# Second expert stage of a two-block transformer kernel: inner columns dealt to partitions in runs of eleven

## The chip, the cores and the metric

The kernel runs on one core of one Trainium2 chip. The metric is the device time of one execution in microseconds (us); lower is better. Engines: PE is TensorE's matmul, PEld its weight load, DVE VectorE, ACT ScalarE, POOL GpSimd, SP the engine whose queue issues most DMAs. L12 is line 12 of the kernel.

## The reference

Two transformer blocks run over 256 tokens of width 1024, all in f32. The first has 32 experts of inner width 512. The second has a dense layer and then an expert layer with 8 experts of inner width 2816, two of them per token. The change touches only this last expert layer:

```python
def _moe_swiglu(u, w_router, w_gate, w_up, w_down):
    ...
    top_logits, top_idx = lax.top_k(logits, TOP_K)          # 2 of 8 experts
    top_w = jax.nn.softmax(top_logits, axis=-1)
    ...
    h = jax.nn.silu(lax.ragged_dot(xs, w_gate, group_sizes)) * lax.ragged_dot(xs, w_up, group_sizes)
    ys = lax.ragged_dot(h, w_down, group_sizes) * top_w.reshape(-1)[order][:, None]
    out = jax.ops.segment_sum(ys, tok, num_segments=n_tok)
```

w_gate and w_up are 8 x 1024 x 2816, w_down is 8 x 2816 x 1024. Their 277 MB are read from DRAM once.

## The kernel before, in words

Each expert is worked in two halves of its inner width: 1408 columns, as 11 tiles of 128 (TH = 11). A half is numbered n = 2e + v. The weights of a half are held in one region of SBUF (the ring of the earlier stages, used here as flat memory): held_gate and held_up hold four k-slices each (KQ = 4, 1408 columns each; a quarter), held_down holds 11 rows of 1024.

TensorE's program for a half (second_slots): half_in runs twice (kk = 0, 1) over the four gate slices and the four up slices. For each slice k it goes over the 11 tiles f of columns and two groups of 64 of them (c = 0, 1), with 64 weight columns as the stationary operand and the 80 token slots of the expert (x_rows) as the moving one. Such a slice, 22 matmuls, is called a piece here. half_down then takes the 11 rows f of held_down with the hidden values hid2 of the half before: 16 matmuls for each row (8 tiles of the output width, two groups of 64). Products are accumulated in PSUM: gate, up and y. After every odd half come the turning of y, the dispatch of the next expert's tokens and the combination into x. For each piece and for each row, TensorE raises the semaphore piece_used.

SP's queue loads the weights in a fixed order: for each half, the eight pieces of quarter 0, the 11 rows of down, and the eight pieces of quarter 1 (each expert: load_quarters, load_downs, load_quarters, twice). Before each DMA, SP waits until piece_used tells that the place is free. A piece is one DMA of 704 KB (128 partitions x 5632 bytes). A row of down is one DMA of 512 KB: partition p of row f receives row f x 128 + p of w_down's half, 4096 bytes; each of the 11 has its own semaphore down_row[f], on which TensorE waits before that row.

ScalarE copies x_rows for each slice (L746), applies silu to gate (L739); VectorE multiplies (L1466), clears PSUM (L1455), and does the combination (L1494, L1500, L1508). All matmuls are issued by the helper at L1824, the transposes by that at L1832.

There is a second form of the stage (second_all, for inputs where an expert gets more than 80 tokens). It does not run with these inputs; the change is made in it as well.

Of the kernel before, what the change touches and what calls it, by code (L numbers as in the profile page):

```python
# [13 lines left out]
P = 128  # L14
HALF = 64
D = 1024
KD = D // P
T = 256
# [23 lines left out]
FH = F2 // 2  # L42
TH = FH // P
KQ = KD // 2
QUARTER = KQ * FH
BANK_TILES = 6
PER_HALF = 4 * KQ + TH


def used_by(n, k):  # L50


    first = isinstance(n, int) and n == 0
    return n * PER_HALF + (k + 1 - (0 if first else TH))

# [73 lines left out]
def build(nc, a, out):  # L129
    with ExitStack() as ctx:  # L130
# [3 lines left out]
        def sem(name):  # L134
            return ctx.enter_context(nc.semaphore(name))
# [121 lines left out]
        x_rows = view(2048, KQ, CAP2)  # L257
# [6 lines left out]
        ps = ctx.enter_context(nc.psum_tensor("ps", [P, 8, CH], F32))  # L264
# [5 lines left out]

        gate_row = [sem(f"gate_row{k}") for k in range(KQ)]
        up_row = [sem(f"up_row{k}") for k in range(KQ)]
        down_row = [sem(f"down_row{f}") for f in range(TH)]
        piece_used = sem("piece_used")
        gate_clear, y_clear = sem("gate_clear"), sem("y_clear")
        rows_ready = sem("rows_ready")
# [48 lines left out]
        GATE_AT, UP_AT, DOWN_AT = 0, QUARTER, 2 * QUARTER  # L325
        held_gate = flat[:, GATE_AT:UP_AT].rearrange("p (k n) -> p k n", k=KQ)
        held_up = flat[:, UP_AT:DOWN_AT].rearrange("p (k n) -> p k n", k=KQ)
        held_down = flat[:, DOWN_AT:DOWN_AT + TH * D].rearrange("p (f n) -> p f n", f=TH)
# [30 lines left out]
        def _(sp):  # L359
# [32 lines left out]
            def expert_rows(w, e, c0, n):  # L392
                return w[bass.ds(e, 1), c0:c0 + n, :].rearrange("o (k p) n -> p (o k) n", p=P)
# [9 lines left out]
            w = a["w_in"][0]  # L403
# [57 lines left out]
            wg, wu, wd = a["moe_w_gate_2"][0], a["moe_w_up_2"][0], a["moe_w_down_2"][0]  # L461

            def left_by_ring(end):
                sp.wait_ge(ring_free, MOE2_SEQ - len(SUMMED) - SLOTS + 1 + (end - 1) // SLOT)
# [14 lines left out]

            def load_downs(e, v, n):  # L480

                for f in range(TH):
                    if n is None:
                        left_by_ring(DOWN_AT + (f + 1) * D)
                    else:
                        sp.wait_ge(piece_used, used_by(n - 1, 4 * KQ + f))
                    sp.dma_start(held_down[:, f, :], expert_rows(wd, e, v * FH, FH)[:, f, :]).then_inc(down_row[f], 16)

            load_quarters(0, 0, 0, None)
            load_downs(0, 0, None)  # L490
# [1324 lines left out]
        def _(pe):  # L1815
# [5 lines left out]
            def mm(*args, **kw):  # L1821


                ins = pe.matmul(*args, **kw)  # L1824
                if owed[0]:
                    ins.then_inc(owed_to[0], owed[0])
                    owed[0] = 0
                    return None
                return ins
# [196 lines left out]
            w = slot(s, KD, CH)  # L2026
            for g in range(2):
                bank = gv_()
                for i in range(2):
                    for k in range(KD):  # L2030
                        for half in range(2):
                            c0 = half * GROUP_HEADS * HD + (2 * g + i) * HD
                            last = mm(ps[half * HALF:(half + 1) * HALF, bank, i * T:(i + 1) * T], w[:, k, c0:c0 + HD],
                                      hT[:, k, :], start=(k == 0), stop=(k == KD - 1))
# [30 lines left out]
            for part in range(2):  # L2065
                turned = gv_()
                for i in range(4):
                    last = sums_turn(4 * part + i, turned, 4 * i)
# [9 lines left out]
            for t in range(TT):  # L2078
                bank = gv_()
                for g in range(4):  # L2080
                    last = mm(ps[:, bank, g * P:(g + 1) * P], gv[:, t, g * P:(g + 1) * P], wsT[:, g, :],
                                     start=True, stop=True)
                last.then_inc(v_full, 1)
            bank = gv_()
            for i in range(4):
                last = sums_turn(8 + i, bank, 4 * i)
# [4 lines left out]
            for g in range(6):  # L2091
# [3 lines left out]
                for i in range(nh):  # L2095
# [3 lines left out]
                    last = mm(ps[:, bank, i * keys:(i + 1) * keys], qT[base:base + HD, j, q0:q0 + P],  # L2099
                                     kT[base:base + HD, 0:keys], start=True, stop=True)  # L2100
# [11 lines left out]
            for blk in range(2):  # L2112
                pe.wait_ge(H["pT_ready"], 2 + 4 * blk)
                bank = gv_()
                for hd in range(HEADS):
                    base, kv = HD * (hd % 2), hd // GROUP_HEADS
                    dst = ps[base:base + HD, bank, (hd // 2) * P:(hd // 2 + 1) * P]
                    if blk == 0:
                        last = mm(dst, v_tok[:, 0, kv * HD:(kv + 1) * HD],
                                         pT[:, hd // 4, (hd % 4) * P:(hd % 4 + 1) * P], start=True, stop=True)  # L2120
                    else:
                        for kt in range(2):
                            at = (2 * (hd % 2) + kt) * P
                            last = mm(dst, v_tok[:, kt, kv * HD:(kv + 1) * HD],
                                             pT[:, 2 + hd // 2, at:at + P], start=(kt == 0), stop=(kt == 1))
# [99 lines left out]
            def second_all(q):  # L2225

                def part_in(n, kk):
                    for which, (w, full) in enumerate(((held_gate, gate_row), (held_up, up_row))):
                        for k in range(KQ):
                            pe.wait_ge(full[k], n * 32 + 16 * (kk + 1))  # L2230
                        for j, (lo, hi) in enumerate(dense_spans):
                            at = n * (4 * len(dense_spans)) + ((2 * kk + which) * len(dense_spans) + j)
                            if not isinstance(at, int) or at:
                                pe.wait_ge(sum_free, at)
                            for f in range(lo, hi):
                                for k in range(KQ):
                                    last = mm(ps[:, 4 + which, (f - lo) * T:(f - lo + 1) * T], w[:, k, f * P:(f + 1) * P],
                                              hT[:, kk * KQ + k, :], start=(k == 0), stop=(k == KQ - 1))
                            last.then_inc(sum_full, 1)
                        free(KQ, piece_used)  # L2240

                def half_in(n):
                    part_in(n, 0)
                    part_in(n, 1)

                def half_down(n, opens):
                    pe.wait_ge(q["hid_ready"], n)
                    for f in range(TH):
                        pe.wait_ge(down_row[f], n * 16)
                        for t in range(TT):  # L2250
                            for half in range(2):
                                last = mm(ps[:, 2 * t + half, :], dense_hid[:, f, t * P:(t + 1) * P],
                                          held_down[:, f, half * CH:(half + 1) * CH],
                                          start=(opens and f == 0), stop=(not opens and f == TH - 1))
                        last.then_inc(piece_used, 1)

                half_in(0)
                half_in(1)
                half_down(1, True)
                with pe.Fori(1, NE2) as i:  # L2260
                    half_in(i * 2)
                    half_down(i * 2, False)
                    half_in(i * 2 + 1)
                    pe.wait_ge(q["y_free"], i)
                    half_down(i * 2 + 1, True)
                half_down(2 * NE2, False)
                pe.wait_ge(q["y_free"], NE2)
# [95 lines left out]
            def second_slots(q, cap):  # L2363

                def quarter(w, full, n, kk, bank):
                    for k in range(KQ):
                        pe.wait_ge(rows_ready, n * (2 * KQ) + (kk * KQ + (k + 1)))
                        pe.wait_ge(full[k], n * 32 + (kk * 16 + 16))
                        for f in range(TH):
                            at = f % BANK_TILES * cap  # L2370
                            for c in range(2):
                                last = mm(ps[c * HALF:(c + 1) * HALF, bank + f // BANK_TILES, at:at + cap],
                                          w[:, k, f * P + c * HALF:f * P + (c + 1) * HALF], x_rows[:, k, :],
                                          start=False, stop=(k == KQ - 1), skip_group_check=True)
                        last.then_inc(piece_used, 1)
                    return last
# [8 lines left out]
                def half_down(n, y_cleared):  # L2385

                    pe.wait_ge(y_clear, y_cleared)
                    for f in range(TH):
                        pe.wait_ge(down_row[f], n * 16)
                        if f % BANK_TILES == 0:  # L2390
                            pe.wait_ge(q["hid_ready"], n * 2 + (f // BANK_TILES - 1))
                        for dt in range(KD):
                            for c in range(2):
                                last = mm(ps[c * HALF:(c + 1) * HALF, Y_BANK + dt // 4, (dt % 4) * cap:(dt % 4 + 1) * cap],
                                          held_down[:, f, dt * P + c * HALF:dt * P + (c + 1) * HALF],
                                          hid2[:, f * cap:(f + 1) * cap], start=False, stop=(f == TH - 1),
                                          skip_group_check=True)
                        last.then_inc(piece_used, 1)
# [102 lines left out]
            for layer in range(2):  # L2501
# [4 lines left out]
                if layer == 0:  # L2506
# [5 lines left out]
                    for c in range(9, ADA_CHUNKS):  # L2512
                        last = ada_turn(1, c, bank, 4 * (c - 8))
# [12 lines left out]
                w = slot(s, KD, CH)  # L2526
# [9 lines left out]
                for t in range(TT):  # L2536
                    last = mm(ps[:, bank, t * T:(t + 1) * T], glT[:, t * P:(t + 1) * P], gkw2[:, :],
                                     start=True, stop=True)
# [30 lines left out]
                for c in range(3):  # L2569
                    bank, rb, t = gv_(), CK * (c % 2), c // 2  # L2570
                    for hd in range(GH):
                        ob, f = DK * (hd % 2), hd // 2
# [119 lines left out]
```

## Time and profile before

| | us |
|---|---|
| median of 3 runs | 2091.62 |
| lowest, highest | 2085.76, 2098.47 |
| the profiled execution, in all | 2094.6 |
| its span | 2092.9 |

The mean granted clock of TensorE was 0.974 of full speed. The profile is one execution. Its page gives busy times and the chain that ended last; the trace behind it answers questions on a stretch, a line or a queue. "busy" of a group is the time in which at least one of its instructions ran; matmuls overlap, so their mean duration is much longer than the distance from one to the next, which is the busy time over their count. A row of the timeline is a run of like instructions: start, length, and the count behind the x; behind it, in brackets, the idle time before it and what ended it.

### The profile page before, as it was taken

Reading aid. Unit: us, or ns where it says so; the run is one execution under the profiler, and the core shown is the slowest. Engines: PE = TensorE matmul, PEld = TensorE weight load, DVE = VectorE, ACT = ScalarE, POOL = GpSimd, SP = SyncE. Lnnn points to the kernel's source line nnn. Section 1 sums busy time; section 2 is a strip of 40 time slices with the busy share of each in tenths; the row PEclk is TensorE's granted clock in tenths of the full one; section 3 lists DMA queues with packets and bytes.
Section 4 is the critical chain, followed back from the end, with each engine's and each line's share of the span. In section 5 each row is a group of like instructions: output and inputs, shape, how many; then the busy total and the mean of one; then the engine's idle time right before and its main releaser. Section 6 shows DMA issues by size and latency. Waiting matters only on the chain.

```text
span 2092.9 us, 67815 instructions
## 1 busy us (share of the span) xinstructions
PE 1985.1 (95%) x31049; PEld 1596.1 (76%) x31049; DVE 650.7 (31%) x1410; ACT 170.2 (8%) x370; POOL 17.3 (1%) x66
## 2 busy tenths in 40 slices
PE   6999899999999989999999999898999999999996
PEld 4787477877787757758677576688898989889894
DVE  4686332232232241354323523600211011110104
ACT  2002010000000011000000110110000000000000
POOL 1000000000000000000000000000000000000000
PEclk9999999999999999999999999999999999999997
DMA  9998559999999993346757433299999999999991
GB/s 351 320 389 311 227 202 418 421 421 422 424 421 421 422 370 144 121 143 249 272 206 262 180 108 133 99 413 384 402 359 379 416 365 413 375 370 412 360 358 74
DMA packets 179138, 655.98 MB, mean 313 GB/s; under 512 B 16212, under 2 KB 20724, under 8 KB 170868
## 3 DMA queue, kind: packets, MB, share of 16 engines
q1 hardware_dynamic: 170528, 647.41, 79.0%
q0 software_dynamic: 1456, 5.24, 0.7%
q10 hardware_dynamic: 7076, 2.20, 0.5%
q8 instruction: 60, 0.98, 0.2%
q14 instruction: 18, 0.15, 0.0%
HBM read 653.76 MB, written 1.05 MB: 313 GB/s over the span
## 4 chain that ended last, share of the span: by engine, by line
PE 89%; DVE 6%; DMA 2%; issue 2%; DVEq 0%; ACT 0%; SPq 0%
PE ps L1824 88%; DMA ring<-in_moe_w_gate_dram 2%; PE ps L1832 1%; DMA ring<-in_w_ada_dram 1%; DVE arena L1494 0%; DVE ps L1455 0%; DVE stat L1100 0%; DVE arena L1300 0%; DVE hT L988 0%; DVE x L1209 0%; DVE tok L975 0%; DVE x L1508 0%; DVE arena L1466 0%; DVE tok L1208 0%; DVE newton L968 0%
## 5 line engine op out<-in xcount | busy, mean ns | idle before, releaser
L1824 PEld LDWEIGHTS ps<-arena,ring 128*64 128x64 f32 (+1 forms) x25216 | 868.6, 139 | 46.2 <-issue 36.3
L1824 PE MATMUL ps<-arena,ring 128*64 128x80 f32 (+2 forms) x25216 | 885.8, 232 | 18.8 <-issue 15.0
L1824 PE MATMUL ps<-hT,ring 128*128 128x256 f32 (+1 forms) x1680 | 361.2, 387 | 4.3 <-DVE stat L992 2.2
L1824 PEld LDWEIGHTS ps<-hT,ring 128*128 128x128 f32 (+1 forms) x1680 | 309.4, 189 | 51.7 <-issue 2.6
L1824 PE MATMUL ps<-ring,arena 128*64 128x512 f32 (+1 forms) x880 | 273.8, 595 | 1.5 <-DVE stat L1732 1.1
L1824 PE MATMUL ps<-arena 128*128 128x128 f32 (+7 forms) x1288 | 231.9, 347 | 27.9 <-DVE x L1508 12.5
L1824 PEld LDWEIGHTS ps<-ring,arena 128*64 128x64 f32 (+1 forms) x880 | 104.5, 159 | 150.8 <-issue 147.2
L1824 PEld LDWEIGHTS ps<-arena 128*128 128x128 f32 (+4 forms) x1288 | 154.5, 191 | 84.9 <-issue 32.5
L1455 DVE MEMSET ps<- 128x480 f32 x68 | 28.9, 425 | 294.3 <-ACT arena L739 290.0
L1824 PE MATMUL ps<-ring,hT 128*128 128x512 f32 (+2 forms) x256 | 87.6, 500 | 0.0
L1824 PEld LDWEIGHTS ps<-ring,hT 128*128 128x128 f32 x256 | 46.1, 190 | 38.1 <-issue 36.2
L1373 DVE TENSOR_TENSOR arena<-arena,ps 128x256 f32<-128x256 f32 x32 | 13.5, 421 | 179.3 <-PE ps L1824 179.3
L1300 DVE SCALAR_TENSOR_TENSOR arena<-arena,csT 128x512 f32<-128x512 f32 x84 | 63.2, 752 | 3.0
L1057 DVE SCALAR_TENSOR_TENSOR arena<-ring,csT,arena 128x512 f32<-128x512 f32 x84 | 63.2, 752 | 3.0
L746 ACT ACTIVATE arena<-arena 128x80 f32<-128x80 f32 x96 | 25.9, 270 | 372.0 <-PE ps L1824 372.0
L1466 DVE TENSOR_TENSOR arena<-arena,ps 128x480 f32<-128x480 f32 (+1 forms) x32 | 18.2, 609 | 121.8 <-PE ps L1824 120.8
L1359 DVE TENSOR_TENSOR x<-x,ps 128x512 f32<-128x512 f32 x68 | 46.8, 688 | 18.9 <-PE ps L1824 18.9
L1392 DVE TENSOR_TENSOR arena<-ps,gB 128x512 f32<-128x512 f32 x32 | 20.6, 686 | 101.4 <-PE ps L1824 101.4
L1494 DVE COPY arena<-ps 80x512 f32<-80x512 f32 x16 | 11.0, 687 | 124.3 <-PE ps L1832 123.4
L717 ACT ACTIVATE arena<-ps 128x256 f32<-128x256 f32 x32 | 12.3, 384 | 437.0 <-PE ps L1824 437.0
L1351 DVE COPY arena<-ps 128x512 f32<-128x512 f32 x34 | 23.5, 692 | 46.5 <-PE ps L1824 46.5
L1832 PEld LDWEIGHTS ps<-ident,arena 128*128 128x128 f32 (+1 forms) x156 | 18.3, 135 | 21.9 <-issue 17.2
(324 smaller groups left out, 796.7 us busy)
## 6 DMA issues: line engine op xcount, KB each, us to landing
ring<-in_moe_w_gate_dram SPq DMA_DIRECT2D x128, 704.0 KB, 8.3
ring<-in_moe_w_up_dram SPq DMA_DIRECT2D x128, 704.0 KB, 9.4
ring<-in_moe_w_down_dram SPq DMA_DIRECT2D x176, 512.0 KB, 10.4
ring<-in_w_gate_dram SPq DMA_DIRECT2D x32, 2048.0 KB, 14.8
ring<-in_w_up_dram SPq DMA_DIRECT2D x32, 2048.0 KB, 14.1
ring<-in_w_down_dram SPq DMA_DIRECT2D x32, 2048.0 KB, 12.3
ring<-in_w_in_dram SPq DMA_DIRECT2D x19, 2048.0 KB, 13.7
ring<-in_w_ada_dram SPq DMA_DIRECT2D x12, 2048.0 KB, 15.6
```

The costliest lines, as they stand in the source:

```text
L717: act.activation(silu_g[:, j % 2, 0:n], ps[:, 6, 0:n], ACT.Silu).then_inc(q["silu_done"], 1)
L746: act.activation(x_rows[:, k, :], xT[:, c * KQ + k, 0:CAP2], ACT.Copy).then_inc(rows_ready, 1)
L1057: ins = dve.scalar_tensor_tensor(out=part, in0=src, scalar=csT[:, m, k:k + 1], in1=part, op0=ALU.mult, op1=ALU.add)
L1300: ins = dve.scalar_tensor_tensor(out=part, in0=src, scalar=csT[:, 1, k:k + 1], in1=part, op0=ALU.mult, op1=ALU.add)
L1351: side_free(q, banks, dve.tensor_copy(xT[:, 4 * c:4 * c + 4, 0:width], ps[:, b, 0:4 * width].rearrange("p (a b) -> p a b", a=4)), i, k + c)
L1359: side_free(q, banks, dve.tensor_tensor(dst, dst, ps[:, b, :], ALU.add), i, k + c)
L1373: dve.tensor_tensor(hid[:, j % 2, 0:n], silu_g[:, j % 2, 0:n], ps[:, 7, 0:n], ALU.mult)\
L1392: ins = dve.tensor_tensor(y_slot[0:width, cols], ps[0:width, 4 + half, :], gB[0:width, 1, cols], ALU.mult)
L1455: ins = dve.memset(ps[:, bank + b, 0:n], 0.0)
L1466: dve.tensor_tensor(hid2[:, at:at + n], gated2[:, at:at + n], ps[:, UP_BANK + b, 0:n], ALU.mult)\
L1824: ins = pe.matmul(*args, **kw)
L1832: ins = pe.transpose(*args)
```

## The change

The inner columns of a half are dealt to the 128 partitions in another order. Before, tile f holds columns f x 128 to f x 128 + 127. After, partition p holds the eleven columns 11p to 11p + 10, and tile f is the set of columns 11p + f. For w_down this makes the 11 rows of a partition one contiguous stretch of 44 KB in DRAM; they are loaded in three DMAs of 4, 4 and 3 rows (16, 16 and 12 KB per partition), each with one semaphore and one wait on piece_used for the last of its rows. The gate and up weights are loaded as before; the matmuls read them as stationary operand with a step of 11 elements (44 bytes), 64 columns at a time. The order of hidden values is the same on both sides of the product, so that nothing else changes.

```diff
+DOWN_GROUPS = ((0, 4), (4, 8), (8, 11))
...
-        down_row = [sem(f"down_row{f}") for f in range(TH)]
+        down_rows = [sem(f"down_rows{g}") for g in range(len(DOWN_GROUPS))]
...
             def load_downs(e, v, n):
 
-                for f in range(TH):
+                src = wd[bass.ds(e, 1), v * FH:(v + 1) * FH, :].rearrange("o (p f) n -> p (o f) n", p=P)
+                for g, (lo, hi) in enumerate(DOWN_GROUPS):
                     if n is None:
-                        left_by_ring(DOWN_AT + (f + 1) * D)
+                        left_by_ring(DOWN_AT + hi * D)
                     else:
-                        sp.wait_ge(piece_used, used_by(n - 1, 4 * KQ + f))
-                    sp.dma_start(held_down[:, f, :], expert_rows(wd, e, v * FH, FH)[:, f, :]).then_inc(down_row[f], 16)
+                        sp.wait_ge(piece_used, used_by(n - 1, 4 * KQ + hi - 1))
+                    sp.dma_start(held_down[:, lo:hi, :], src[:, lo:hi, :]).then_inc(down_rows[g], 16)
...
# second_slots, quarter
                             for c in range(2):
                                 last = mm(ps[c * HALF:(c + 1) * HALF, bank + f // BANK_TILES, at:at + cap],
-                                          w[:, k, f * P + c * HALF:f * P + (c + 1) * HALF], x_rows[:, k, :],
+                                          w[:, k, bass.ds(c * HALF * TH + f, HALF, TH)], x_rows[:, k, :],
                                           start=False, stop=(k == KQ - 1), skip_group_check=True)
...
# second_slots, half_down
                     for f in range(TH):
-                        pe.wait_ge(down_row[f], n * 16)
+                        pe.wait_ge(down_rows[f // 4], n * 16)
```

second_all gets the same two edits: `w[:, k, bass.ds(f, P, TH)]` and `down_rows[f // 4]`.

## Rows read from the trace of the kernel before

**Rows 1.** The page: busy time per engine and the chain that ended last.

```profile
PE 1985.1 (95%) x31049; PEld 1596.1 (76%) x31049; DVE 650.7 (31%) x1410; ACT 170.2 (8%) x370; POOL 17.3 (1%) x66
...
PE ps L1824 88%; DMA ring<-in_moe_w_gate_dram 2%; PE ps L1832 1%; DMA ring<-in_w_ada_dram 1%; DVE arena L1494 0%; DVE ps L1455 0%; DVE stat L1100 0%; DVE arena L1300 0%; DVE hT L988 0%; DVE x L1209 0%; DVE tok L975 0%; DVE x L1508 0%; DVE a
```

**Rows 2.** Groups by shape, 1360 to 2093 us: busy us, mean ns | idle before.

```profile
L1824 PE MATMUL ps<-arena,ring 128*64 128x80 f32 x16642 | 603.6, 235 | 17.0 <-issue 15.0 <-DMA ring<-in_moe_w_gate_dram 0.9 <-ACT arena L746 0.3
```

**Rows 3.** Timeline of TensorE: start us, length us, what.

```profile
1607.57 37.02 PE L1824 MATMUL ps<-arena,ring 128*64 128x80 f32 x1056 [0.87 <-issue]
1644.78 38.36 PE L1824 MATMUL ps<-arena,ring 128*64 128x80 f32 x1056 [0.19 <-issue]
...
1822.34 12.39 PE L1824 MATMUL ps<-arena,ring 128*64 128x80 f32 x352 [0.19 <-issue]
1835.23 26.13 PE L1824 MATMUL ps<-arena,ring 128*64 128x80 f32 x704 [0.49 <-DMA ring<-in_moe_w_gate_dram]
...
2002.96 38.49 PE L1824 MATMUL ps<-arena,ring 128*64 128x80 f32 x1056 [0.19 <-issue]
```

**Rows 4.** Windows of two combines: length, PE busy, granted clock, DMA share, GB/s.

```profile
1595.00:1607.50 12.50, 9.57 (x68) 1.00 1.03 409
1683.00:1695.50 12.50, 10.38 (x54) 0.87 1.03 409
```

**Rows 5.** Windows of one expert: length, granted clock, DMA share, GB/s.

```profile
1607.50:1612.50 5.00, 1.00 0.51 164
1612.50:1620.00 7.50, 1.00 0.95 339
1620.00:1632.50 12.50, 1.00 1.02 422
1635.00:1650.00 15.00, 1.00 1.02 412
```

**Rows 6.** Windows of the first expert stage, the same columns.

```profile
520.00:530.00 10.00, 1.00 1.01 406
530.00:550.00 20.00, 1.00 1.01 428
```

**Rows 7.** Waits of SP's queue, 1350 to 2093 us: total us, times, longest.

```profile
SPq L487 <- PE ps L1824: 112.5, 165, 14.5
```

**Rows 8.** Timeline of SP's queue, the down loads of an even half.

```profile
1633.56 11.54 SPq L487 DMA_DIRECT2D ring<-in_moe_w_down_dram  x11
```

**Rows 9.** Issue to landing: an even half's first down, an odd half's, all pieces.

```profile
ring<-in_moe_w_down_dram SPq DMA_DIRECT2D x1, 512.0 KB, 8.9
...
ring<-in_moe_w_down_dram SPq DMA_DIRECT2D x11, 512.0 KB, 12.8
...
DMA to landing us min/median/max: 3.9/9.5/12.0
```

**Rows 10.** Groups by shape over the whole span, TensorE.

```profile
L1824 PE MATMUL ps<-arena,ring 128*64 128x64 f32 x8192 | 245.2, 222 | 0.9 <-DVE arena L1351 0.9
...
L1824 PE MATMUL ps<-arena 128*128 128x80 f32 x288 | 34.2, 277 | 3.1 <-DVE arena L1494 2.4 <-DVE arena L1444 0.7
...
L1824 PE MATMUL ps<-table,arena 128*64 128x32 f32 x256 | 7.8, 223 | 0.0
```

**Rows 11.** One line in a stretch, ScalarE's strided copies: ns min/median/max.

```profile
L785 ACT ACTIVATE arena<-ps x4: 1063/1092/1102, 261.7 to 264.4; 128x512 f32<-128x512 f32 x4
```

**Rows 12.** Timeline of ScalarE, the same line with a contiguous destination.

```profile
1338.81 0.60 ACT L785 ACTIVATE arena<-ps 128x512 f32<-128x512 f32 x1 [4.77 <-PE ps L1832]
```

**Rows 13.** VectorE reading PSUM with a step of 32 bytes, and contiguous.

```profile
L941 DVE TENSOR_TENSOR arena<-ps,band_mask x6: 680/691/692, 27.4 to 71.2; 128x512 f32<-128x512 f32 x6
...
L1698 DVE COPY arena<-ps 128x512 f32<-128x512 f32 x4 | 2.8, 692 | 9.4 <-PE ps L1824 9.4
```

More of the change, by code:

```diff
@@ L2236, in part_in @@
                                 for k in range(KQ):
-                                    last = mm(ps[:, 4 + which, (f - lo) * T:(f - lo + 1) * T], w[:, k, f * P:(f + 1) * P],
+                                    last = mm(ps[:, 4 + which, (f - lo) * T:(f - lo + 1) * T], w[:, k, bass.ds(f, P, TH)],
                                               hT[:, kk * KQ + k, :], start=(k == 0), stop=(k == KQ - 1))
@@ L2388, in half_down @@
                     for f in range(TH):
-                        pe.wait_ge(down_row[f], n * 16)
+                        pe.wait_ge(down_rows[f // 4], n * 16)
                         if f % BANK_TILES == 0:
```

## The prediction, made before the changed kernel was run

> **What bounds the kernel now.** I read first the page (busy shares, the chain that ended last), then the second expert stage alone: its groups by shape, the timeline of TensorE, the timeline of SP's queue, the DMA rate in short windows, and the time from issue to landing. The page says that TensorE is busy for 95% of the span and that 88% of the chain runs through its matmul line [rows 1]. But a busy TensorE need not be at its own pace; the question is which of TensorE and DMA ends last in the stage that changes.
>
> That stage runs from 1351 us to 2068 us. Its expert matmuls are 16,896 instructions, and those that the window holds are busy for 603.6 us [rows 2]. The number tells how a matmul appears: 16 halves x (352 gate and up + 176 down) = 8,448 calls, and twice as many MATMULs, so each f32 matmul is two weight loads and two MATMULs. A piece (one k of gate or up: 22 calls, 44 instructions) and a row of down (16 calls, 32 instructions) run at one pace where nothing is waited for: 352 instructions in 12.39 us [rows 3], 35.2 ns each. A half is 1,056 of them, 37.2 us; two halves and about 12.3 us of turning, dispatch and combine give 86.7 us per expert. The bytes of an expert are 34.6 MB, at 415 GB/s 83.4 us. The two are nearly level, and the trace shows who is ahead where:
>
> - In the even half after the combine, TensorE is never short of data: 37.02 us for 1,056 [rows 3]. (Other even halves take 1 to 2 us more; there the granted clock had fallen in the combine before them, where TensorE idles. It shows 0.87 in one of these stretches, against 1.00 in another [rows 4]. The change doesn't touch that.)
> - In the odd half it is a little short: 38.36 us, 38.49 us, and 39.0 us from 1822.34 to 1861.36 [rows 3], 1.2, 1.3 and 1.8 us above 37.2. These are the least, the last and the most of the six odd halves from 1556 us on, which lose 9.2 us in all. One names a gate load as what was waited for [rows 3]. This is where DMA decides.
> - The queue runs empty once per expert, after the combine: 164 GB/s in 1607.5 to 1612.5 and 339 in the next 7.5 us, then 412 to 422 [rows 5].
>
> **The change part by part.**
>
> *The rows of down land in longer runs.* Before, each of 11 DMAs brings 4 KB per partition; after, three bring 16, 16 and 12 KB contiguous from DRAM. The first expert stage shows both forms: its gate and up loads are 16 KB per partition, its down loads 4 x 4 KB. The rate is 428 GB/s in a window of the former and 406 in one of the latter [rows 6], and so on in turn. In the second stage down's rows come at 412 [rows 5]. A half's down load is 11 x 524,288 B = 5.77 MB: 14.0 us at 412, 13.5 us at 428, so 0.5 us less. It counts only where the queue decides. The down load issued in the even half stands in the queue ahead of the gate and up pieces that the odd half is short of; the one issued in the odd half is followed by the empty queue, and its gain is idle time. So six odd halves x 0.5 = 3.2 us, and 0.5 us for the DMA-bound start of the stage: 3.7 us. Bounds: 0, and 9.2 us, all that the odd halves now lose.
>
> *Eight issues fewer per half.* SP's queue spends 0.33 us on each; before down's rows alone it waits 112.5 us for TensorE [rows 7], so nothing is gained. TensorE's eleven waits per half stay eleven.
>
> *SP waits for four rows instead of one.* The first group of down can go only when row 3 is used: three rows of 32 x 35.2 ns = 1.13 us later, 3.4 us. Behind this wait on SP's queue stand the other two groups and then the next pieces. The last group waits for row 10 exactly as the last DMA did, so the pieces behind it go out when they did. The delay is hidden while the queue holds over 3.4 us of work. The first down load of the even half is issued at 1633.56 [rows 8] and lands 8.9 us later [rows 9]; its own bytes take 1.3 us, and the fixed part is about 2.2 us (the quickest 704 KB load lands in 3.9 us [rows 9], of which 1.7 us are its bytes). That leaves 5.4 us of queued work, 2 us more than the delay. Group 0 then works for 5.1 us and group 1 comes 4.5 us behind it, so the cover stays. In the odd half landing takes 12.8 us [rows 9] and the cover is 9.3 us. Cost 0; if that cover were gone, the cost is up to 3.4 us per half. A group that lands whole is late for nobody: the rows are needed more than 20 us after they are issued, and at the end of the stage, too, the combine lies between.
>
> *The weight loads of gate and up step over 11 columns (44 bytes).* This is 5,632 calls, 11,264 weight loads. No row of the trace shows a weight load with a step, so I bound it. What a load may cost unseen: with 64 moving columns the same loads pass at 245.2 us / 8,192 = 29.9 ns, and with 32 at 7.8 / 256 = 30.5 ns [rows 10], so about 30 ns per instruction is the pace that 64-column loads allow; with 80 moving columns it is 35.2. A load may become 17% longer before anything is lost. The 128-column form agrees: 34.2 us / 288 = 119 ns, two times 59 [rows 10]. The nearest rows with a step are of other engines. ScalarE's copies of 512 elements take 1,092 ns with a destination step of 512 B [rows 11] and 0.60 us contiguous [rows 12]: factor 1.83. VectorE, reading PSUM with a step of 32 B, needs 691 ns for 512 elements [rows 13], as much as its contiguous copies (692 ns [rows 13]): factor 1. The ends are thus 0 and, with 1.83 x 29.9 = 54.7 ns, 19.5 ns x 11,264 = 220 us; a full doubling gives 59.8 ns and 277 us. Below zero is excluded: the columns are as many as before. I take 0. The weight load is a read, and the row that is a strided read shows no loss; the strided row that loses is a write, with a step that is more than eleven times as long. But it is a choice between ends far apart, and it carries most of the uncertainty.
>
> Here the Trainium skill speaks against the change: Advanced Engine Details and Errata, SBUF Cachelines, says that SBUF has lines of 16 bytes, that an engine needs at least two hits on a line for full performance, and that a new line for each access costs a penalty. A step of 44 bytes never hits a line twice. By that rule the sum would be the second rival's; by the VectorE row it is the forecast. No run here shows the rule for TensorE so far.
>
> *Sum.* -3.7 + 0 + 0 + 0 = -3.7 us against the profiled execution: 2094.6 us in all (span 2092.9 and 1.7 around it), so 2090.9. The median of the three runs is 2091.6, 3.0 us under the profiled one; put on it, the change gives 2087.9, say 2088 us.
>
> **The rivals.**
>
> 1. *The strided load sets the pace.* For it: the pace of gate and up has only 17% of room, and ScalarE's strided copies lose 1.83. Against it: VectorE's row. Place: every gate and up piece, from 44 x 35.2 = 1.55 us to 44 x 54.7 = 2.4 us or 44 x 59.8 = 2.6 us. It decides from 35.2 ns per instruction on. Then TensorE alone is the bound, the 9 us of the odd halves vanish: 2092 + 220 - 9 = 2303 to 2092 + 277 - 9 = 2360 us. Chance 0.30. The cacheline rule above would end here.
> 2. *A smaller penalty,* 36 to 45 ns per instruction: 0.8 to 9.8 ns x 11,264 = 9 to 110 us less up to 9, so 2092 to 2193 us. Nothing in the rows speaks for a size between; chance 0.10.
> 3. *The group waits empty the queue.* If the 2 us of cover is misjudged, up to 3.4 us of idle queue per even half, eight times: up to 27 us less the 4 gained, some 2115; likelier 0.5 us each, 2092. Against it: the landing times. Chance 0.08, mostly within the bound.
> 4. *The transfer is hidden anyway:* 2091.6; or the odd halves lose their whole stall: 2082. Both belong to the forecast's case, 0.52.
>
> **How the numbers follow.** A change of 0.5% is 10.5 us, about what the measurement of this kernel can tell from none; its three runs spread over 12.7 us. In the forecast's own case (0.52) the time is 2078 to 2098: the bounds 2082 and 2092 and the spread of a median; 0.10 of it faster than the 0.5%, 0.42 within. Rival 3 gives 0.05 within and 0.03 slower, rival 2 0.01 within and 0.09 slower, rival 1 0.30 slower. Faster 0.10, same 0.48, slower 0.42. The range for 8 in 10 has to reach into rival 1: 2078 leaves out 0.04 below, 2345 some 0.12 above.
>
> **What would show it.** Right: 352 gate and up instructions still in 12.4 us, and groups of 64-column loads with 80 moving columns near 36 ns; 48 down DMAs; 425 to 430 GB/s where down's rows flow; odd halves at 37.7 to 38.2 us; no window of low DMA between an even half's first down row and the next pieces. Wrong: pieces longer than 1.6 us, with ScalarE's copies of x_rows spaced accordingly, a DMA rate below 380 GB/s throughout, and down rows still at 1.13 us each (down's weights are not strided) means rival 1 or 2, and the piece gives its price; a dip of the DMA rate 2 to 5 us after TensorE begins down means rival 3.

## The result, and the profile after

The changed kernel takes 2375.59 us (median of 4 runs, 2371.98 to 2378.35) against 2093.01 us for the kernel before (4 runs, 2085.76 to 2098.47): ratio 1.1352, 95% interval 1.1313 to 1.139, or 282.6 us more. The prediction was 2088 us with a range up to 2345 us. The rival "the strided load sets the pace" came about, with a price above the top of its own range.

The page of the changed kernel (lines are 2 higher than before, those of the gate and up loads 1; L1826 is the matmul helper). First busy time, then the chain that ended last, then DMA issues with the median time to landing:

```profile
PE 2274.0 (96%) x31049; PEld 1897.8 (80%) x31049; DVE 650.6 (27%) x1410; ACT 170.3 (7%) x370; POOL 17.5 (1%) x66
...
PE ps L1826 91%; PE ps L1834 1%; DMA ring<-in_w_ada_dram 1%; DVE stat L1102 0%; DVE x L1510 0%; DVE arena L1496 0%; DVE ps L1457 0%; DVE arena L1302 0%; DVE hT L990 0%; DVE x L1211 0%; DVE tok L977 0%; DVE arena L1468 0%; DVE tok L1210 0%; 
...
ring<-in_moe_w_gate_dram SPq DMA_DIRECT2D x128, 704.0 KB, 4.1
ring<-in_moe_w_up_dram SPq DMA_DIRECT2D x128, 704.0 KB, 4.1
...
ring<-in_moe_w_down_dram SPq DMA_DIRECT2D x32, 2048.0 KB, 8.0
```

Against [rows 1], PE has 289 us more busy time from the same number of instructions, and the gate load that took 2% of the chain [rows 1] is no longer in it. The other engines' busy times are as before. Gate and up loads land in 4.1 us, close to the 3.9 us of an unqueued one [rows 9]: most of them wait for nothing in the DMA queue any more.

Groups by shape over the whole span. First the kernel before, then the changed one: the matmuls of the stage, those of the first expert stage, which the change leaves alone, and the weight loads of both stages (844.4 us busy before):

```profile
L1824 PE MATMUL ps<-arena,ring 128*64 128x80 f32 x16896 | 612.5, 235 | 17.0 <-issue 15.0 <-DMA ring<-in_moe_w_gate_dram 0.9 <-ACT arena L746 0.3
...
L1826 PE MATMUL ps<-arena,ring 128*64 128x80 f32 x16896 | 910.3, 272 | 4.9 <-issue 4.9
...
L1826 PE MATMUL ps<-arena,ring 128*64 128x64 f32 x8192 | 245.2, 222 | 0.9 <-DVE arena L1353 0.9
...
L1826 PEld LDWEIGHTS ps<-arena,ring 128*64 128x64 f32 x25088 | 1150.6, 177 | 21.3 <-issue 21.3
```

Busy time of the same 16,896 instructions grows by 297.8 us, idle time ahead of them falls by 12.1 us; together 285.7 us. The stage, from its first to its last expert matmul, is 284.0 us longer in the profiles (1001.0 against 717.0 us), so this is the whole difference. The first expert stage is the same to the tenth.

The timeline of TensorE for an even and an odd half, to be held against [rows 3]; then the last odd half, and down's rows of the last half, behind the last combine:

```profile
1702.94 57.02 PE L1826 MATMUL ps<-arena,ring 128*64 128x80 f32 x1056 [0.64 <-issue]
1760.13 56.77 PE L1826 MATMUL ps<-arena,ring 128*64 128x80 f32 x1056 [0.17 <-issue]
...
2264.16 56.77 PE L1826 MATMUL ps<-arena,ring 128*64 128x80 f32 x1056 [0.22 <-issue]
...
2333.77 13.62 PE L1826 MATMUL ps<-arena,ring 128*64 128x80 f32 x352
```

An odd half takes 56.77 us each time: it is no longer short of data. The timeline of SP's queue shows the piece itself, since SP issues the next load whenever TensorE has used one. First four issues in a row in the kernel before; then, in the changed kernel, a single issue, four in a row, the three groups of down, and the DMA rate of an odd half:

```profile
1736.37 4.89 SPq L474 DMA_DIRECT2D ring<-in_moe_w_gate_dram  x4
...
1691.14 0.33 SPq L489 DMA_DIRECT2D ring<-in_moe_w_down_dram  x1
...
1739.50 8.65 SPq L475 DMA_DIRECT2D ring<-in_moe_w_up_dram  x4
1752.24 8.21 SPq L489 DMA_DIRECT2D ring<-in_moe_w_down_dram  x3
...
1760.00:1820.00 60.00, 1.00 0.86 309
```

A run of four issues holds three distances and one issue of 0.33 us: (8.65 - 0.33) / 3 = 2.77 us for a piece, 63.0 ns for each of its 44 instructions. The kernel before has 4.89 us for the same run, 1.52 us for a piece and 34.5 ns per instruction. All paces below are read in this way. Down's rows keep their pace: 56.77 - 16 x 2.77 = 12.4 us for 352 instructions, 35.2 ns, as before [rows 3]. So each gate and up instruction costs 27.8 ns more than the 35.2 ns of the sum, x 11,264 = 313 us; some 18 us of that were already busy time before (612.5 us against 16,896 x 35.2 ns = 594.7 us, waits for data and stretches of low granted clock among it), and 12 us were idle time.

### The profile page after: what moved, and what is told of

The parts are those of the page before. It is cut to its first block, busy times and chain, and to the rows that moved or that the text cites. A ratio compares the mean times of both kernels' runs of the same rounds, so it can differ in the third digit from the quotient of the medians.

```text
span 2370.2 us, 67351 instructions
## 1 busy us (share of the span) xinstructions
PE 2274.0 (96%) x31049; PEld 1897.8 (80%) x31049; DVE 650.6 (27%) x1410; ACT 170.3 (7%) x370; POOL 17.5 (1%) x66
## 3 DMA queue, kind: packets, MB, share of 16 engines
HBM read 653.76 MB, written 1.05 MB: 276 GB/s over the span
## 4 chain that ended last, share of the span: by engine, by line
PE 92%; DVE 5%; issue 1%; DMA 1%; DVEq 0%; ACT 0%; SPq 0%
PE ps L1826 91%; PE ps L1834 1%; DMA ring<-in_w_ada_dram 1%; DVE stat L1102 0%; DVE x L1510 0%; DVE arena L1496 0%; DVE ps L1457 0%; DVE arena L1302 0%; DVE hT L990 0%; DVE x L1211 0%; DVE tok L977 0%; DVE arena L1468 0%; DVE tok L1210 0%; DVE newton L970 0%; DVE hT L1085 0%
## 5 line engine op out<-in xcount | busy, mean ns | idle before, releaser
L1826 PEld LDWEIGHTS ps<-arena,ring 128*64 128x64 f32 (+1 forms) x25216 | 1174.7, 177 | 25.7 <-issue 22.5
L1826 PE MATMUL ps<-arena,ring 128*64 128x80 f32 (+2 forms) x25216 | 1183.6, 256 | 6.7 <-issue 4.9
L1826 PE MATMUL ps<-hT,ring 128*128 128x256 f32 (+1 forms) x1680 | 357.8, 383 | 4.2 <-DVE stat L994 2.2
L1826 PEld LDWEIGHTS ps<-hT,ring 128*128 128x128 f32 (+1 forms) x1680 | 307.3, 188 | 50.3 <-issue 2.5
L1826 PE MATMUL ps<-ring,arena 128*64 128x512 f32 (+1 forms) x880 | 273.8, 595 | 1.5 <-DVE stat L1734 1.1
L1826 PE MATMUL ps<-arena 128*128 128x128 f32 (+7 forms) x1288 | 224.7, 337 | 27.8 <-DVE x L1510 12.7
L1826 PEld LDWEIGHTS ps<-ring,arena 128*64 128x64 f32 (+1 forms) x880 | 104.5, 159 | 150.8 <-issue 147.2
L1826 PEld LDWEIGHTS ps<-arena 128*128 128x128 f32 (+4 forms) x1288 | 150.7, 186 | 83.2 <-issue 30.1
L1826 PE MATMUL ps<-ring,hT 128*128 128x512 f32 (+2 forms) x256 | 87.6, 500 | 0.0
L1826 PEld LDWEIGHTS ps<-ring,hT 128*128 128x128 f32 x256 | 46.1, 190 | 38.1 <-issue 36.2
## 6 DMA issues: line engine op xcount, KB each, us to landing
ring<-in_w_down_dram SPq DMA_DIRECT2D x32, 2048.0 KB, 12.4
```

## The experiments

Theory 1: the strided weight load alone made the loss. Theory 2: the new way of loading down did, by its coarse groups or by its long runs. The first two runs each keep one half of the change.

**e1_down_alone**: the changed kernel with gate and up read without a step.

```diff
-                                          w[:, k, bass.ds(c * HALF * TH + f, HALF, TH)], x_rows[:, k, :],
+                                          w[:, k, f * P + c * HALF:f * P + (c + 1) * HALF], x_rows[:, k, :],
```

> Down's rows in three contiguous DMAs as in the changed kernel, gate and up weights read without a step (the inner columns of gate and up then no longer match down's rows). Theory 1, the strided weight load alone made the loss: within 0.5% of the kernel before, 2083 to 2093 us, pieces at 1.52 us, odd halves 37.7 to 38.2 us. Theory 2, the loss comes from the way down is loaded (coarse groups, long runs, or both): well above 2150 us.

Measured: 2089.07 us (12 runs) beside 2091.77 us (23 runs), ratio 0.999, interval 0.9973 to 1.0007. Two odd halves, four windows (the ramp after the combine; pieces; 2 to 5 us after TensorE begins down; down's rows), and the three groups of down:

```profile
1640.76 38.42 PE L1826 MATMUL ps<-arena,ring 128*64 128x80 f32 x1056 [0.19 <-issue]
1730.52 38.12 PE L1826 MATMUL ps<-arena,ring 128*64 128x80 f32 x1056 [0.20 <-issue]
...
1603.50:1608.50 5.00, 1.00 0.43 131
1616.00:1630.00 14.00, 1.00 1.02 421
1630.50:1633.00 2.50, 1.00 1.01 415
1637.00:1650.00 13.00, 1.00 1.00 425
...
1632.85 8.21 SPq L489 DMA_DIRECT2D ring<-in_moe_w_down_dram  x3
```

Theory 2 falls. The later issue of down leaves no dip in the DMA rate, and down's rows flow at 425 GB/s instead of 412 [rows 5] (420, 430 and 421 in three other even halves, where before has 410 to 412). The last six odd halves take 37.7 to 38.4 us, against 38.4 to 39.0: 3.8 us less in all, where the sum had 3.2. The 2.7 us between the medians agree with the 3.7 us of the sum, but the interval holds zero as well.

**e2_step_alone**: the kernel before with the step alone (the edit above, the other way round).

> Only the step of 11 on the gate and up weight loads; down's rows in eleven DMAs of 4 KB per partition as before (again the columns do not match down's rows). Theory 1: 2370 to 2380 us like the changed kernel, pieces of 2.77 us. Theory 2: near 2090 us. If both parts are needed (strided reads that collide with long DMA writes): between the two, with pieces shorter than 2.77 us.

Measured: 2383.92 us (4 runs), ratio 1.1397, interval 1.1365 to 1.143; pieces of 2.77 us:

```profile
1661.25 8.65 SPq L474 DMA_DIRECT2D ring<-in_moe_w_up_dram  x4
```

The step alone is the whole loss. It comes out 8 us above the changed kernel; in the profiles the stage itself, from its first to its last expert matmul, takes 1004.8 against 1001.0 us, and starts 10.5 us later, after work that the two have in common. So some of the 8 us lies before the stage and is no effect of the change.

**e3_runs_of_four** and **e4_runs_of_two** compute what the reference asks for, with the columns dealt in shorter runs: each group of down covers its own 512 (384, 256, 128) columns, and its runs are as long as the group has rows.

```diff
+def columns(f, first, n):
+    lo, hi = DOWN_GROUPS[GROUP_OF[f]]
+    return bass.ds(lo * P + first * (hi - lo) + f - lo, n, hi - lo)
...
-DOWN_GROUPS = ((0, 4), (4, 8), (8, 11))
+DOWN_GROUPS = ((0, 2), (2, 4), (4, 6), (6, 8), (8, 10), (10, 11))
...
-                                          w[:, k, bass.ds(c * HALF * TH + f, HALF, TH)], x_rows[:, k, :],
+                                          w[:, k, columns(f, c * HALF, HALF)], x_rows[:, k, :],
```

(Runs of four keep the groups of the changed kernel.)

> Same three down DMAs with 16, 16 and 12 KB per partition, but the runs are of 4, 4 and 3 columns inside each group, so the weight loads step over 4 (16 bytes) or 3 elements instead of 11. If a load is slow only when each element lies in another 16-byte line and a step of exactly 16 bytes counts as free: 2085 to 2093 us. If the pace follows the number of lines touched (64 lines for step 4, 48 for step 3, 16 for step 1): step 4 costs as much as step 11 and step 3 some less, 2300 to 2375 us.

> Runs of two: down in six DMAs, five with 8 KB per partition and one with 4 KB; the weight loads step over 2 elements (8 bytes), in the last tile over 1. Two elements share a 16-byte line. If two hits on a line are enough: pieces at 1.52 us and 2083 to 2093 us, a little under the kernel before by its longer runs. If any step above 1 is slow: near 2340 us.

Measured: runs of four 2297.8 us (5 runs), ratio 1.0989, interval 1.0963 to 1.1015; runs of two 2089.73 us (12 runs), ratio 0.9994, interval 0.9977 to 1.0011. Timelines of SP's queue, first of the runs of four, then of the runs of two:

```profile
1647.34 7.69 SPq L484 DMA_DIRECT2D ring<-in_moe_w_up_dram  x4
```

```profile
1647.90 4.89 SPq L484 DMA_DIRECT2D ring<-in_moe_w_gate_dram  x4
```

A step of 2 costs nothing that shows (1.52 us for a piece); 4 and 3 mixed give 2.45 us. A step of exactly 16 bytes is not free.

**e5_step_three** and **e6_step_five** put one step on all loads of the kernel before; 57 and 51 are only the distances of their starts.

```diff
-                                          w[:, k, f * P + c * HALF:f * P + (c + 1) * HALF], x_rows[:, k, :],
+                                          w[:, k, bass.ds((2 * f + c) * 57, HALF, 3)], x_rows[:, k, :],
```

> The kernel before with a step of 3 elements (12 bytes) on all gate and up weight loads; they read other columns than the reference asks for. From the runs of four, where 12 of 44 instructions of a piece step over 3: (2.45 us - 32 x 63.0 ns) / 12 = 36 ns, so pieces of about 1.6 us and 2090 to 2110 us. If instead each new 16-byte line costs the same, 48 of 64 loads touch a new line: about 56 ns per instruction, pieces of 2.45 us, near 2300 us.

> The same with a step of 5 elements (20 bytes). If from 16 bytes on every step costs the same: 63 ns per instruction, pieces of 2.77 us, 2370 to 2390 us. If the cost grows with the step: between the runs of four (63 ns for step 4) and the step of 11 (63 ns) there is no room, so anything else would point to an odd step or an alignment.

Measured, one run each beside 2088.06 us for the kernel before: 2177.74 and 2315.11 us. Timelines of SP's queue, step 3 and then step 5:

```profile
1699.47 6.22 SPq L474 DMA_DIRECT2D ring<-in_moe_w_gate_dram  x4
```

```profile
1749.96 7.95 SPq L474 DMA_DIRECT2D ring<-in_moe_w_up_dram  x4
```

Both expectations missed. Step 3 is neither free nor at 56 ns: 1.96 us for a piece, 44.6 ns. Step 5 is at 57.7 ns, under step 11. My 36 ns had come from taking 63 ns for step 4 in the mixed run; with 44.6 ns for the 12 instructions of step 3, the other 32 get (2,453 - 535) / 32 = 59.9 ns.

**e7_step_half_moving** and **e8_half_moving**: half the moving columns, with and without the step of 11. The lines show e7 against e2; the width of the output is halved in both as well.

```diff
-                                          w[:, k, bass.ds(c * HALF * TH + f, HALF, TH)], x_rows[:, k, :],
+                                          w[:, k, bass.ds(c * HALF * TH + f, HALF, TH)], x_rows[:, k, 0:cap // 2],
```

> Step of 11 alone, with only 40 of the 80 token slots as the moving operand of gate and up (half of those products are left out). If the weight load alone sets the pace: 63 ns per instruction still, pieces of 2.77 us, 2370 to 2390 us. If load and moving operand add up: 63 - 40 x 0.42 = 46 ns, pieces near 2.0 us, near 2190 us.

> The kernel before with only 40 moving columns in gate and up. The pace that contiguous loads allow, from the rows with 64 and 32 moving columns, is about 30 ns per instruction: pieces of 1.32 us where no DMA is waited for; the whole then bound by DMA, 2070 to 2092 us. If 80 moving columns were not what set 35.2 ns: pieces still 1.55 us and 2092 us.

Measured, one run each: 2383.93 and 2130.35 us. Timelines of SP's queue with the step, and without:

```profile
1659.66 8.63 SPq L474 DMA_DIRECT2D ring<-in_moe_w_up_dram  x4
```

```profile
1747.24 4.18 SPq L474 DMA_DIRECT2D ring<-in_moe_w_gate_dram  x4
```

With the step, (8.63 - 0.33) / 3 = 2.77 us: half the moving columns, the same pace. The weight load alone sets it; load and moving operand do not add up. Without the step, 1.28 us and 29.2 ns where no data is waited for: that is the pace of contiguous loads, and 35.2 ns is the pace of 80 moving columns. The total of the second missed: 2130 us, more than with twice the work. Its odd half shows why; the second row is a run of 704 in an even half:

```profile
1664.91 32.97 PE L1824 MATMUL ps<-arena,ring 128*64 128x40 f32 x704 [4.83 <-DMA ring<-in_moe_w_gate_dram]
1722.70 22.70 PE L1824 MATMUL ps<-arena,ring 128*64 128x40 f32 x704 [0.17 <-issue]
...
1665.00:1698.00 33.00, 33.00 (x706) 0.66 1.02 414
```

TensorE waits 4.8 us for a gate load, and after that the granted clock is 0.66 over the 33 us that follow; 704 instructions then take 33.0 us instead of the 22.7 us that the other run takes, at a granted clock of 1.00. Even halves behind a combine lose in the same way: the one from 1515 us takes 50.7 us, at 0.52 in its first 41 us.

With 40 moving columns the granted clock falls to 0.50, the lower of its two levels, for whole runs of issues, and this shows more of what sets the pace. Runs of four issues and the windows over them, each at 0.50 and then at 1.00; first with the step of 11 (e7), then without (e8):

```profile
1601.32 8.62 SPq L474 DMA_DIRECT2D ring<-in_moe_w_up_dram  x4
1601.00:1610.00 9.00, 9.00 (x149) 0.50 0.83 279
1659.00:1668.00 9.00, 9.00 (x148) 1.00 0.84 280
```

```profile
1527.12 7.37 SPq L474 DMA_DIRECT2D ring<-in_moe_w_up_dram  x4
1527.00:1535.00 8.00, 8.00 (x156) 0.50 0.96 332
1724.00:1729.00 5.00, 5.00 (x179) 1.00 1.02 425
```

Without the step a piece takes 2.35 us at the lower clock and 1.28 us at the higher; with the step of 11 it takes 2.76 us at the lower and 2.77 us at the higher. The strided load does not follow TensorE's clock, so its price is not one that the array pays cycle by cycle.

A theory of pairs came next: a load takes its elements two by two and is slow for each pair that does not share a 16-byte line. It gives 44.6 ns for step 3 from even starts, where every other pair shares a line, and e5 was read as such a run. That reading was wrong: its starts are multiples of 57, so the second group of 64 columns (c = 1) always starts odd, where no pair of step 3 shares a line, and the expectation of e10 repeats the mistake. Three runs put other starts to the theory (edits as in e5: `bass.ds((2 * f + c) * 60 + 2, HALF, 2)`, `... * 56 + 1, HALF, 3)`, `... * 60 + 1, HALF, 1)`).

> The kernel before with a step of 2 elements on gate and up, each load starting at a column that is 2 more than a multiple of 4 (other columns than the reference asks for). Theory of pairs: a load takes its elements two by two, the first with the second, the third with the fourth, and is slow for each pair that does not lie in one 16-byte line. Here every pair straddles two lines: about 58 ns per instruction, pieces of 2.54 us, near 2315 us. Theory of the step alone (8 bytes are free, as in the runs of two, whose starts are 0 or 1 above a multiple of 4): pieces of 1.52 us, 2085 to 2097 us.

> A step of 3 again, but all loads start 1 above a multiple of 4. From there the pairs (1,4), (7,10), (13,16) never share a line, while from the even starts of the earlier run every other pair does. Theory of pairs: 58 ns per instruction, pieces of 2.54 us, near 2315 us. Theory of the step alone: pieces of 1.96 us and 2178 us as before.

> No step, but each load starts 1 above a multiple of 4: the pairs (1,2), (5,6) share a line, (3,4), (7,8) straddle. Theory of pairs taken to its end: half of the pairs are slow, 44 to 45 ns per instruction, pieces of 1.96 us, near 2178 us. If contiguous elements are read by another way (the step alone decides): pieces of 1.52 us, 2085 to 2097 us.

Measured, one run each beside 2092.57 us: 2089.33, 2173.95 and 2095.14 us. Timelines of SP's queue, step 2, step 3 and step 1:

```profile
1649.97 4.90 SPq L474 DMA_DIRECT2D ring<-in_moe_w_up_dram  x4
```

```profile
1658.23 6.17 SPq L474 DMA_DIRECT2D ring<-in_moe_w_up_dram  x4
```

```profile
1654.56 4.90 SPq L474 DMA_DIRECT2D ring<-in_moe_w_up_dram  x4
```

The theory of pairs falls in all three: it wanted pieces of 2.54, 2.54 and 1.96 us. Step 3 takes the same from odd starts as from the mixed ones of e5 (6.17 against 6.22 us). At steps 1 and 2 the 80 moving columns would hide a load that is up to 20% longer (29.2 to 35.2 ns), so for these only a larger effect of the start is excluded.

**e12_step_one_group** asks whether the two groups of 64 columns load side by side. It has the step of 11 and puts both groups into one half of the array.

```diff
-                                last = mm(ps[c * HALF:(c + 1) * HALF, bank + f // BANK_TILES, at:at + cap],
-                                          w[:, k, f * P + c * HALF:f * P + (c + 1) * HALF], x_rows[:, k, :],
+                                last = mm(ps[0:HALF, bank + f // BANK_TILES, at:at + cap],
+                                          w[:, k, bass.ds(c * HALF * TH + f, HALF, TH)], x_rows[:, k, :],
```

> Step of 11 alone, with both groups of 64 columns placed in the same half of the array (the second group's products are added to the first's). If the two halves' loads run side by side today, each at 126 ns: 126 ns per instruction, pieces of 5.5 us, near 3080 us. If one path carries both in turn at 63 ns each: pieces of 2.77 us still and near 2384 us.

Measured, one run: 3088.94 us. Timeline of SP's queue:

```profile
1678.76 16.94 SPq L474 DMA_DIRECT2D ring<-in_moe_w_up_dram  x4
```

That is 5.54 us for a piece, 126 ns per instruction. One load of 64 columns at step 11 takes 126 ns; the kernels above run two at a time. Loads of 63 ns in turn, each followed by its matmul, would not give this: without a step a load and its matmul fit into 2 x 35.2 = 70.4 ns in one half of the array, which beside a load of at least 29.2 ns leaves the matmul 41.2 ns at most, and 63 + 41.2 is 104 ns.

So the cost per load is twice the pace: 58.4 ns at step 1 (with 40 moving columns), 89.2 at step 3, 119.8 at step 4, 115.4 at step 5, 126 at step 11. 64 columns touch 16, 48, 64, 64 and 64 lines of 16 bytes. The three last give 1.87, 1.80 and 1.97 ns per line, and step 3 gives 1.86 for its 48. A theory of lines: a load takes the longer of 64 elements at 0.91 ns and its lines at some 1.85 ns. Two runs test it, one on a point where no cover hides the load, one on the other operand. (Not shown in the lines: e13 halves the output as e7 does. e14 reads another tile of SBUF as its moving operand.)

```diff
+# e13_step_two_half_moving
+                                          w[:, k, bass.ds((2 * f + c) * 60, HALF, 2)], x_rows[:, k, 0:cap // 2],
...
+# e14_moving_step_four
+                                          w[:, k, f * P + c * HALF:f * P + (c + 1) * HALF], h_tok[:, k % 2, bass.ds(4 * k, cap, 4)],
```

> Step of 2 with 40 moving columns in gate and up (half of the products left out), so that nothing hides the load. Theory of lines (a load needs the greater of 64 elements at 0.91 ns and the touched 16-byte lines at 1.85 ns): 32 lines, 59 ns for a load, 29.6 ns per instruction, pieces of 1.28 to 1.31 us like the kernel with step 1 and 40 moving columns, and 2125 to 2135 us like it. Theory of a cost that grows with the step (29.2 at 1, 44.6 at 3): 34 to 37 ns, pieces of 1.5 to 1.63 us.

> Weight loads without a step, but the moving operand of gate and up is 80 columns of another tile in SBUF, read with a step of 4 elements (16 bytes); the products are meaningless. If the moving operand pays for lines like a load: 80 x 1.85 = 148 ns per instruction of each half of the array, 74 ns per instruction, pieces of 3.3 us, near 2520 us. If only weight loads pay: pieces of 1.52 us, 2085 to 2097 us.

Measured, one run each beside 2096.63 us: 2140.42 and 2484.3 us. Timelines of SP's queue:

```profile
1663.47 4.28 SPq L474 DMA_DIRECT2D ring<-in_moe_w_up_dram  x4
```

```profile
1712.23 9.83 SPq L474 DMA_DIRECT2D ring<-in_moe_w_up_dram  x4
```

Step 2 without cover: 1.32 us, 29.9 ns, against 29.2 at step 1; the theory of lines said 29.6. The moving operand at step 4: 3.17 us, 72.0 ns, the theory said 74. Both paces hold within 3%, though 1.32 us is just above its band of 1.28 to 1.31. The totals held less well: 2484 us against some 2520, and 2140 us above its band by the same kind of stretch as in e8 (runs of four issues of 7.37 us at a granted clock of 0.50, beside those of 4.28). That the step costs e14 its time and not the other tile was not run apart.

| step | bytes | 16-byte lines of 64 columns | piece, us | ns per instruction | kernel, us |
|---|---|---|---|---|---|
| 1 | 4 | 16 | 1.52 (1.28 with 40 moving) | 34.5 (29.2) | 2093 |
| 2 | 8 | 32 | 1.52 (1.32 with 40 moving) | 34.5 (29.9) | 2089, 2090 |
| 3 | 12 | 48 | 1.96 | 44.6 | 2178, 2174 |
| 4 (8 tiles) and 3 (3 tiles) | 16, 12 | 64, 48 | 2.45 | 59.9 for step 4 | 2298 |
| 5 | 20 | 64 | 2.54 | 57.7 | 2315 |
| 11 | 44 | 64 | 2.77 | 63.0 | 2376, 2384 |

## Why the prediction was wrong

- **What bounds the kernel** held: TensorE's pace by a little, DMA only in the odd halves. That is why a longer piece went straight into the total.
- **Longer runs of down** (-3.7 us): in size right. e1 shows 425 GB/s in place of 412, and a median 2.7 us lower, with an interval of -0.27% to +0.07%. The total can't be told from no change. The mechanism shows in the odd halves, 3.8 us shorter together, where the sum had 3.2; the stage itself was 6.5 us shorter in its profile (710.5 against 717.0 us), one execution each.
- **Fewer issues, and the wait for four rows**, both at 0: right. In e1 the down groups find the queue still filled (415 GB/s in the 2.5 us before the first is issued, 425 from 4 us after it).
- **The step of 11 columns** at 0: this failed. The sentence "a load may become 17% longer before anything is lost" was right (29.2 to 35.2 ns is 20%, and step 2 stays inside), and so was its own row for the pace of contiguous loads. Wrong was the choice between the two strided rows: I took VectorE's [rows 13], because it is a read, over ScalarE's [rows 11], whose time per strided element turned out near that of the weight load: 1.8 ns for a strided element of ScalarE (1,092 ns less 170 fixed, over 512), 1.97 ns for one of the load. (Its contiguous copies of 512 and 256 elements take 598 and 384 ns in the trace of the kernel before: 0.84 ns per element and 170 ns fixed.) VectorE's row reads PSUM, so it could say nothing of a read of SBUF. (Its speed is no excuse: 692 and 491 ns for 512 and 320 elements are 1.05 ns per element and 156 ns fixed, under the 1.8 ns of a strided element.) That ScalarE's write and TensorE's read of SBUF pay for the same cause is not shown; only the times agree. Measured: 63.0 ns, 27.8 ns above 35.2, 313 us less some 30 us that were waits, low clock or idle before; 284 us in the stage.
- **The rival's price** was too low: I bounded it with a full doubling, 59.8 ns, and took off 9 us for the odd halves. The load of step 11 is 2.16 times the contiguous one (63.0 over 29.2). The 9 us were too few as well: some 30 us of waits, low clock and idle time went, since the strided load hides not only the odd halves' stall but also the start of the stage and the low clock after a combine (an even half that begins at a granted clock of 0.50 takes 38.6 us before, 1.6 us more than one at 1.00, and 57.0 us after, 0.3 us more). The factor of ScalarE's whole instruction, 1.83, contains its fixed part; per element it is 2.15 (1.80 over 0.84), which would have given 64 ns. The range ended at 2345 us by choice, inside the rival's 2303 to 2360; the measured 2376 us lie above both.
- **The rule of the Trainium skill** (Advanced Engine Details and Errata, SBUF Cachelines: two hits on a 16-byte line are needed for full performance) agrees with every run: step 2 has two hits and is all but free (29.9 ns against 29.2), step 3 has 1.33 and pays in part (44.6 ns), step 4 and above have one and pay in full (57.7 to 63.0 ns). I had it and gave it the smaller chance on the strength of a row of another memory. The prediction calls its sum once that of the second rival; the rival that it belongs to is the first, as the prediction says there.

The mechanism "the cost follows the lines touched" is shown for steps 1 to 5, it forecast the pace of two runs within 3%, and it fits that the strided load takes the same at half the granted clock (e7). Open: why step 11 costs 1.97 ns per line where steps 4 and 5 cost 1.87 and 1.80; a step between 5 and 11 was not run, nor a power of two above 4. Whether a 128-column load with 256 moving columns would hide the step was not tried either; the form of the stage that has it does not run with these inputs.

No version here beats both kernels by more than the measurement can tell. Runs of two give down 8 KB per partition at no price on TensorE and end at 0.9994 of before; full runs of eleven need the step of eleven with this layout, and their gain in DMA is at most the few us of e1.

## What to carry to other kernels

The weight operand of a matmul could be read from SBUF with a step for nothing only while two of its elements shared a 16-byte line: for f32 that is step 2, and where the moving operand is the slower one it hides a little more (6 ns per instruction here). The moving operand was tried at step 4 alone, and paid. Before trading a strided read on the busiest engine for a better DMA, compare both sides in the same unit: here 0.5 us per half of DMA time, mostly hidden, against 16 pieces x 1.25 us on the path. And when two rows of other engines bound an unknown price, take the one with the same memory, and compare per element, after its fixed part is taken off; here that row was within a tenth.

## What the runs showed of the hardware that was not expected

- Loads into the two halves of the array run side by side, each at its own pace: 126 ns for one of 64 columns at step 11, 63 ns per instruction for two halves (e12 against e2).
- A strided weight load does not follow TensorE's clock: a piece takes 2.76 us at a granted clock of 0.50 and 2.77 us at 1.00 (e7), where a piece without a step takes 2.35 and 1.28 us (e8).
- The moving operand pays about the same price per line as the weight load: 72.0 ns x 2 / 80 = 1.80 ns per element at step 4 (e14), against 0.88 ns at the most without a step (35.2 ns x 2 / 80).
- The start of a load does not matter for step 3: 1.95 us for a piece from odd starts (e10), 1.96 from mixed ones (e5). Contiguous loads that begin one element into a line keep 1.52 us (e11), where the moving operand could hide up to 6 ns per instruction.
- A shorter piece made the kernel slower: with 40 moving columns TensorE waits for DMA, the granted clock is then 0.66 over 33 us, and the runs end at 2130 us (e8) and 2140 us (e13), 2% above the kernel before.
